# FFN gate and up products with the weight tile as the stationary operand and 256 token columns moving

## What is computed

```python
def _rmsnorm(x, g):
    y = x32 * lax.rsqrt(jnp.mean(x32 * x32, axis=-1, keepdims=True) + NORM_EPS)
    return (y * g.astype(jnp.float32)).astype(x.dtype)
def _swiglu(h, w_gate_up, w_down):
    gu = jnp.einsum('bsd,df->bsf', h, w_gate_up)
    g, u = gu[..., :FF], gu[..., FF:]
    return jnp.einsum('bsf,fd->bsd', jax.nn.silu(g) * u, w_down)
...
    for layer in range(DEPTH):
        hn = _rmsnorm(h, norm_mix[layer])
        h = h + _mixer(hn, w_in[layer], w_ret_o[layer], w_sb_o[layer], w_out[layer])
        hn = _rmsnorm(h, norm_ffn[layer])
        h = h + _swiglu(hn, w_gate_up[layer], w_down[layer])
```

## Time and profile before

| | |
|---|---|
| time before, median of 3 runs | 2092.74 us (2091.91 to 2096.03) |
| the profiled execution's own time | 2091.68 us |
| its span, first to last instruction | 2089.5 us |
| PE busy | 2070.0 us, 99% of the span |
| PE weight loads busy | 1684.9 us, 81% |
| DVE busy | 1234.4 us, 59% |
| ACT busy | 1113.5 us, 53% |
| granted TensorE clock | 1.000 of full speed |

### The profile page before, as it was taken

How to read it: one execution, slowest core, us unless ns; L and a number is a source line. 1 busy time by engine, 2 the same in 40 slices (tenths; PEclk the granted TensorE clock), 3 DMA queues, 4 the chain that set the end, 5 groups by cost and what they waited for, 6 DMA issues and landing times.

```text
span 2089.5 us, 25155 instructions
## 1 busy us (share of the span) xinstructions
PE 2070.0 (99%) x9627; PEld 1684.9 (81%) x9627; DVE 1234.4 (59%) x1721; ACT 1113.5 (53%) x1682; POOL 36.4 (2%) x60
## 2 busy tenths in 40 slices
PE   8999999999999999999999999999999999999999
PEld 7877888888778888888877888888888888788887
DVE  6576665565666655555567765655555466655553
ACT  6565444445665544644456665544444465665442
POOL 0000100000000000000000000000000000000000
PEclk9999999999999999999999999999999999999999
DMA  7545566555455665565554344565565653445553
GB/s 249 160 142 161 177 191 182 182 174 167 143 161 182 200 186 188 177 193 182 182 166 136 131 152 148 177 189 182 183 187 185 183 190 131 172 140 162 183 187 125
DMA packets 258214, 359.76 MB, mean 172 GB/s; under 512 B 16908, under 2 KB 152288, under 8 KB 258096
## 3 DMA queue, kind: packets, MB, share of 16 engines
q1 hardware_dynamic: 256016, 352.75, 53.6%
q0 software_dynamic: 2080, 5.41, 0.8%
HBM read 357.04 MB, written 1.06 MB: 171 GB/s over the span
## 4 chain that ended last, share of the span: by engine, by line
PE 96%; DVE 2%; ACT 1%; issue 1%; POOL 0%; DMA 0%; SPq 0%; DVEq 0%; ACTq 0%
PE M L780 29%; PE M L782 28%; PE M L781 28%; PE AUX L822 3%; PE AUX L836 1%; DVE WL L1270 1%; PE AUX L1022 1%; PE AUX L1000 1%; PE AUX L947 1%; ACT WH L1049 0%; PE AUX L962 0%; PE AUX L874 0%; PE AUX L953 0%; DVE RET L1453 0%; PE AUX L988 0%
## 5 line engine op out<-in xcount | busy, mean ns | idle before, releaser
L1270 DVE TENSOR_TENSOR WL<-RAW,WH 128x1024 fp32r<-128x1024 f32 x669 | 815.8, 1222 | 669.7 <-ACT WH L1049 666.9
L1049 ACT ACTIVATE WH<-RAW 128x1024 fp32r<-128x1024 f32 x669 | 706.5, 1058 | 680.7 <-PE M L782 674.8
L780 PE MATMUL M<-WH,Bh 128*128 128x512 f32 x1792 | 720.5, 402 | 2.3 <-DVE WL L1270 2.3
L782 PE MATMUL M<-WH,Bl 128*128 128x512 f32 x1792 | 700.8, 391 | 0.0
L781 PE MATMUL M<-WL,Bh 128*128 128x512 f32 x1792 | 699.1, 390 | 0.0
L782 PEld LDWEIGHTS M<-WH,Bl 128*128 128x128 f32 x1792 | 336.8, 188 | 73.2
L780 PEld LDWEIGHTS M<-WH,Bh 128*128 128x128 f32 x1792 | 337.2, 188 | 71.8 <-DVE WL L1270 3.4
L781 PEld LDWEIGHTS M<-WL,Bh 128*128 128x128 f32 x1792 | 337.8, 188 | 63.7
L1078 ACT ACTIVATE AS<-M,KEEP 128x256 f32<-128x256 f32 x132 | 55.4, 471 | 101.1 <-PE M L782 97.6
L780 PE MATMUL M<-WH,MTh 128*128 128x512 f32 x128 | 55.2, 431 | 0.0
L782 PE MATMUL M<-WH,MTl 128*128 128x512 f32 x128 | 50.6, 396 | 0.0
(11 more groups left out here) (405 smaller groups left out, 2525.1 us busy)
## 6 DMA issues: line engine op xcount, KB each, us to landing
RAW<-in_ffn_w_in SPq DMA_DIRECT2D x352, 256.0 KB, 3.2
RAW<-in_w_in SPq DMA_DIRECT2D x104, 512.0 KB, 3.5
RAW<-in_w_gate_up SPq DMA_DIRECT2D x176, 256.0 KB, 3.2
RAW<-in_ffn_w_out SPq DMA_DIRECT2D x88, 512.0 KB, 3.6
RAW<-in_w_down SPq DMA_DIRECT2D x44, 512.0 KB, 3.6
RAW<-in_x_w_kv SPq DMA_DIRECT2D x32, 512.0 KB, 3.5
RAW<-in_even_w_in SPq DMA_DIRECT2D x24, 512.0 KB, 3.8
RAW<-in_odd_w_in SPq DMA_DIRECT2D x24, 512.0 KB, 3.9
```

Of the source, the lines that this page charges most:

```text
L780: e.matmul(out, s.hi, wh, start=s.at0, stop=False)
L782: i = e.matmul(out, s.lo, wh, start=False, stop=s.final)
L1049: e.activation(p.WH[:, h, 0:s.size], p.RAW[:, i, 0:s.size], ACT.Copy).then_inc(k.w_hi, 1)
L1270: e.tensor_tensor(p.WL[:, h, 0:s.size], p.RAW[:, s.u % NRAW, 0:s.size], hi.bitcast(F32), ALU.subtract).then_inc(k.w_lo, 1)
```

## The change

The gate and up products swap their operands. For each k-tile, a 128x128 block of the weights is stationary and all 256 tokens of B move. A chunk's bank 0 gets the 256 gate features (two blocks of 128 features, 256 tokens each) and bank 1 the 256 up features, with features on the partitions. That is 8 x 4 x 3 = 96 products of 256 columns where there were 48 of 512. The result is already turned, and the four transposes of a chunk go.

Since tokens now lie along the free axis, the factor r can't be a scalar per partition any more. A new step `rb` makes one 128x256 tile RB per FFN: PE multiplies r, broadcast along the free axis, by the identity (two 128x128 products), and ACT copies the bank to RB. DVE `ff` multiplies the gate bank by RB, ACT takes its silu, DVE `fh` multiplies the up bank (without r) by it, ACT rounds to Ah, and DVE `fl` subtracts to make Al. The up half's factor r is moved behind the down products, where it is a scalar per partition again (`rs`, r times the FFN's factor of 1.0 or 0.5, in `res`). The buffers HB are changed in shape, and the memory and the final gain go into the TMP tiles, which makes room for RB.

```diff
-    "conv": (0.0, 0.9), "turn": (0.5, 1.0), "tq": (0.5, 0.0), "gains": (0.5, 1.0), "rope": (0.0, 0.6), "ff": (0.0, 0.5),
+    "conv": (0.0, 0.9), "turn": (0.5, 1.0), "tq": (0.5, 0.0), "gains": (0.5, 1.0), "rope": (0.0, 0.6), "ff": (0.7, 0.0), "fh": (0.7, 0.0), "rb": (0.4, 0.0),
...
+    def chunk_w(self, name, region, nk, lab):
...
+                for half in range(2):
+                    s = self.add("mw", self.now + 0.5 * half, 3)
+                    s.c, s.kt, s.u, s.kk, s.t, s.ncol = c, kt, u, kk, half, ncol
...
+                    s.hi, s.lo = (x[:, kt, :] for x in region)
...
-            s.c, s.half, s.scale = c, n, scale
+            s.c, s.half, s.rb = c, n, rb
...
     def ffn(self, gate, down, lab_in, lab_mid, scale, gain, lab_next, A, HB, final=False):
+        nm = self.norms[lab_in]
+        rb = self.add("rb", nm.at + 3.5)
+        rb.norm, rb.scale, rb.rs = nm, scale, self.small(T)
+        past = [None, None]
         for c_ in range(FF // 256):
-            c = self.chunk(gate, self.B, 0, KD, lab_in)
+            c = self.chunk_w(gate, self.B, KD, lab_in)
             s = self.add("ff", c.end, 0)
-            s.c, s.norm, s.i = c, self.norms[lab_in], c_
-            s.silu = [self.AS[:, (c_ % 2) * 2 + t, 0:256] for t in range(T)]
-            s.h = [HB[:, (c_ % 3) * 2 + t, :] for t in range(T)]
-            blocks = [s.h[t][:, q * P:(q + 1) * P] for q in range(2) for t in range(T)]
-            self.turn(c.end + 2.0, "bank", s, blocks, A, 2 * c_, None, lab_mid, 2 * c_)
-        self.residual(down, A, KF, lab_mid, scale, gain, lab_next, final=final)
+            f = self.add("fh", c.end + 1.2)
+            o = self.add("fl", c.end + 2.6)
+            s.c, s.rb, s.past, s.g = c, rb, past[c_ % 2], HB[:, c_ % 2, :]
+            f.c, f.s, f.past, f.h = c, s, past[c_ % 2], HB[:, 2 + c_ % 2, :]
+            o.f = f
+            f.hi, o.lo = (x[:, 2 * c_:2 * c_ + 2, :].rearrange("p k c -> p (k c)") for x in A)
+            past[c_ % 2] = o
+            for q in range(2):
+                self.made[lab_mid, 2 * c_ + q] = o
+        self.residual(down, A, KF, lab_mid, rb, gain, lab_next, final=final)
...
+        elif s.kind == "mw":
...
+            for j in range(2):
+                out = p.M[c.banks[s.t]][:, 256 * j:256 * j + 256]
+                at = s.kk * s.ncol + 256 * s.t + P * j
+                wh, wl = (x[:, h, at:at + P] for x in (p.WH, p.WL))
+                e.matmul(out, wh, s.hi, start=s.at0 and j == 0, stop=False)
+                e.matmul(out, wh, s.lo, start=False, stop=False)
+                i = e.matmul(out, wl, s.hi, start=False, stop=s.final and j == 1)
+            if s.unit_end:
+                i.then_inc(k.w_used, 1)
+        elif s.kind == "rb":
+            e.wait_ge(k.r_made, s.norm.n)
...
+            for t in range(T):
+                i = e.matmul(aux[:, t * P:(t + 1) * P], s.norm.r[:, t:t + 1].to_broadcast([P, P]), ident, start=True, stop=True)
+            i.then_inc(k.aux_full[b], 1)
...
         elif s.kind == "ff":
             table = "s"
-            for t in range(T):
-                e.activation(s.silu[t], banks[t][:, 0:256], ACT.Silu, scale=r[t]).then_inc(k.silu_made, 1)
+            e.wait_ge(k.m_out[s.c.banks[0]], s.c.use[0])
+            e.activation(s.g, s.g, ACT.Silu).then_inc(k.silu_made, 1)
+        elif s.kind == "fh":
+            e.wait_ge(k.m_out[s.c.banks[1]], s.c.use[1])
+            e.activation(s.hi, s.h, ACT.Copy).then_inc(k.ff_hi, 1)
+        elif s.kind == "rb":
+            e.wait_ge(k.aux_full[b], s.use)
+            e.activation(p.RB, aux[:, 0:T * P], ACT.Copy).then_inc(k.aux_out[b], 1)
...
         elif s.kind == "ff":
-            for t in range(T):
-                e.wait_ge(k.silu_made, 2 * (s.n - 1) + t + 1)
-                e.scalar_tensor_tensor(out=s.h[t], in0=banks[t][:, 256:512], scalar=r[t], in1=s.silu[t], op0=ALU.mult,
-                                       op1=ALU.mult).then_inc(k.m_out[c.banks[t]], 1)
...
+            e.tensor_tensor(g, m, p.RB.unsqueeze(1).to_broadcast([P, 2, T * P]), ALU.mult).then_inc(k.m_out[c.banks[0]], 1)
+        elif s.kind == "fh":
...
+            e.tensor_tensor(s.h, banks[1][:, :], s.s.g, ALU.mult).then_inc(k.m_out[c.banks[1]], 1)
+        elif s.kind == "fl":
+            e.wait_ge(k.ff_hi, s.f.n)
+            e.tensor_tensor(s.lo, s.f.h, s.f.hi.bitcast(F32), ALU.subtract).then_inc(k.ff_lo, 1)
```

More of the change, by code:

```diff
@@ L263, in chunk @@
         return c
+    def chunk_w(self, name, region, nk, lab):
+        self.bank_use[2 * self.pair] += 1
+        self.bank_use[2 * self.pair + 1] += 1
+        c = Chunk(name, self.pair, [self.bank_use[2 * self.pair], self.bank_use[2 * self.pair + 1]])
+        self.pair ^= 1
+        kt = 0
+        while kt < nk:
+            u = self.unit(name)
+            kn, ncol, _ = self.units[u]
+            for kk in range(kn):
+                for half in range(2):
+                    s = self.add("mw", self.now + 0.5 * half, 3)
+                    s.c, s.kt, s.u, s.kk, s.t, s.ncol = c, kt, u, kk, half, ncol
+                    s.at0, s.final = kt == 0, kt == nk - 1
+                    s.unit_end = half == 1 and kk == kn - 1
+                    s.src = self.made[lab, kt]
+                    s.hi, s.lo = (x[:, kt, :] for x in region)
+                    c.mms.append(s)
+                kt += 1
+                self.now += 1
+            c.done = u + 1
+        c.end = self.now
+        return c
     def unit(self, name):
@@ L643, in odd_mixer, with memory_turn @@
             self.add("cv_lo", c.end + 6.3 + 2.0 * f).y = y
-    def memory_turn(self, l, at, MX, MT):
+    def memory_turn(self, l, at, MT):
         ss = self.small(4)
         ld = self.add("memld", at)
-        ld.done, ld.MX = self.n_unit + 1, MX
+        ld.done = self.n_unit + 1
+        MX = [[self.TMP[2 * t + n] for n in range(2)] for t in range(T)]
         for n in range(2):
@@ L651, in memory_turn @@
                 k = 4 * n + 2 * j
-                blocks = [MX[:, t, (k + q) * P:(k + q + 1) * P] for q in range(2) for t in range(T)]
+                blocks = [MX[t][n][:, (2 * j + q) * P:(2 * j + q + 1) * P] for q in range(2) for t in range(T)]
                 g = [self.gain(32 + l * 40 + 24 + k + q) for q in range(2)]
                 self.turn(at + 12 + 3 * n + 1.5 * j, "mem", ld, blocks, MT, k, g, f"mt{l}_", k).kt_half = n
-            sq = self.squares(at + 13.5 + 3 * n, "mem", ld, n, [MX[:, t, n * 512:(n + 1) * 512] for t in range(T)], ss)
+            sq = self.squares(at + 13.5 + 3 * n, "mem", ld, n, [MX[t][n] for t in range(T)], ss)
         self.norm(at + 18, f"mt{l}_", sq, ss)
@@ L784, in tensor @@
                 i.then_inc(k.w_used, 1)
+        elif s.kind == "mw":
+            c = s.c
+            h = s.u % NHL
+            if s.kk == 0 and s.t == 0:
+                e.wait_ge(k.w_lo, s.u + 1)
+            if s.src not in seen:
+                seen.add(s.src)
+                e.wait_ge(k.aux_out[s.src.bank], s.src.use)
+            if s.at0 and c.use[s.t] > 1:
+                e.wait_ge(k.m_out[c.banks[s.t]], c.use[s.t] - 1)
+            for j in range(2):
[9 more added lines that the diff above has]
+            e.wait_ge(k.r_made, s.norm.n)
+            if s.use > 1:
+                e.wait_ge(k.aux_out[b], s.use - 1)
+            for t in range(T):
+                i = e.matmul(aux[:, t * P:(t + 1) * P], s.norm.r[:, t:t + 1].to_broadcast([P, P]), ident, start=True, stop=True)
+            i.then_inc(k.aux_full[b], 1)
         elif s.kind == "narrow":
@@ L1256, in vector @@
             aux = p.AUX[b]
-        if s.kind in ("ff", "ch", "res", "mer1", "mer2"):
+        if s.kind in ("ff", "fh", "ch", "res", "mer1", "mer2"):
             c = s.c
@@ L1558, in vector @@
                 x = p.X[:, t, s.half * 512:(s.half + 1) * 512]
-                q = e.scalar_tensor_tensor(out=x, in0=x, scalar=r[t], in1=p.NF[:, s.half * 512:(s.half + 1) * 512], op0=ALU.mult, op1=ALU.mult)
+                q = e.scalar_tensor_tensor(out=x, in0=x, scalar=r[t], in1=p.TMP[4 + s.half], op0=ALU.mult, op1=ALU.mult)
             q.then_inc(k.x_fin, 1)
@@ L1664, in gpsimd @@
                 for t in range(T):
-                    e.dma_start(s.MX[:, t, n * 512:(n + 1) * 512],
+                    e.dma_start(p.TMP[2 * t + n],
                                 a["mem_2"][0, t * P:(t + 1) * P, n * 512:(n + 1) * 512]).then_inc(k.d_mem[s.n - 1][n], 16)
@@ L1669, in gpsimd @@
             for n in range(2):
-                e.dma_start(p.NF[:, n * 512:(n + 1) * 512],
+                e.dma_start(p.TMP[4 + n],
                             a["norm_final"][n * 512:(n + 1) * 512].unsqueeze(0).to_broadcast([P, 512])).then_inc(k.d_nf, 16)
@@ L1788, in build_program @@
                     else:
-                        MX = sb("MXa", [P, T, D], F32, c)
-                        p.memory_turn(0, p.now, MX, MT)
-                        p.NF = MX[:, 0, :]
+                        p.memory_turn(0, p.now, MT)
```

42 lines of the change are left out of this document (30 added, 12 removed).

## The result

| | before | after |
|---|---|---|
| median of 4 runs, us | 2092.85 (2091.91 to 2096.03) | 2107.67 (2106.78 to 2109.83) |
| span of the profiled execution, us | 2089.5 | 2105.0 |

The ratio is 1.007, 95% interval 1.0052 to 1.0087. The change costs 14.8 us; the forecast was a gain of 20.5. The time is the one that the first rival, *The load takes from the stream*, gave: 2106.7 us.

The account below looks back on a forecast made before the run. PE's instruction stream was taken as the bound. Products and turns -25.2, RB +2.7, wait at `rb` +3.2 and vanished waits -1.2 gave -20.5 us: 2072.2 us from 2092.7, range 2062 to 2126, the forecast's own 2062 to 2081.

Parts of the forecast that it names:

- The load takes from the stream: Rival at every gate and up product: 120.0 ns a step, +14.0 us in all, 2106.7 us; chance 0.25.
- What bounds the kernel: PE's instruction stream: busy 2070.0 of 2089.5 us at full clock, to be read by distances from start to start.
- s: Start-to-start distance of a new 256-column gate or up product behind a full load, taken as 114.5 ns, range 111 to 126.7.
- third point: Plain float32 products on PE: nearly equal stream and full load overlap with 2 or 3 ns of loss.
- fourth: fp32r products of 384 columns behind full loads: 175 ns, 15 over the stream, which would suggest s of 120.0 ns.
- The products' and turns' term: Gate and up chunks on PE: 96 products at 114.5 ns against 11.374 us, times 66 chunks, -25.2 us.
- The argument against that rival: On gate and up products: the surcharge with hardly any load is already half of that at 512 columns.
- RB: Two plain float32 products of 128 columns per FFN on PE, 0.45 us, six times: +2.7 us.
- Wait at `rb`: PE waits once for r, in the first FFN, where POOL's DMA issues precede the norm: +3.2 us.
- Waits for HB: PE's wait in the first FFN, 0.8 us, and a smaller one in the second block go: -1.2 us.
- Turns: Four transposes per gate and up chunk on PE, with what they disturb: 0.49 us of a chunk's 11.374.
- DVE and ACT at zero: Their FFN work, at most 7.0 and 6.4 us of an 11 us chunk, was to add nothing.

Follow-up runs that it names:

- e8: Changed kernel with only 64 of 128 weight columns loaded per gate and up product in six of eight k-tiles: 2079.93 us, 113.5 ns a step.
- e7: Changed kernel with POOL's 17 DMA issues of the first FFN put behind the norm: 2102.27 us, one run.
- e4: Kernel before without the FFN's turns, ACT and DVE splitting the gated rows untransposed: 2059.76 us, ratio 0.9843.
- e5: Changed kernel with Bh and Bl moved in one 512-column product behind one load, and POOL's first-FFN DMA issues behind the norm: 2085.98 us, ratio 0.9967.
- e11: Changed kernel with only 96 of 128 weight columns loaded per gate and up product in six of eight k-tiles: 2089.93 us, 116.3 ns a step.
- e9: Kernel before with only 32 token columns loaded beside 512 moving columns in six of eight gate and up k-tiles: 2102.86 us, 231.7 ns a step.

## Why the prediction was wrong

**What bounds the kernel, and the way to read it**: right. PE sets the end in both, at full clock, and only the distance from start to start tells the time. The durations would have misled: 284 ns a product, 192 a load.

**The step that failed is the choice of s.** The prediction took 114.5 ns, "the 113.3 ns of the earlier trace rows with about half of the 2 or 3 ns that the closely matched pair in the earlier trace rows loses". It held that a full load is hidden behind a full-speed stream of 256 columns but for 1 or 2 ns. Measured are 120.0. Its third point, plain float32, was given more weight than its fourth, fp32r behind full loads. The fourth had the right number, 13.3 ns on each product; that the full load takes all of it holds for half at most (e8). The earlier trace rows is a stream at half speed; that a load hides there says nothing of a stream at full speed. The earlier trace rows is a load of 8 columns, and e8 shows that it stands for loads up to 64, not for a full one. The products' and turns' term was thus -25.2 us and came out at 66 x (11.52 - 11.374) = +9.6. The prediction gave that outcome as a rival with 0.25, though it says itself why is no test of a full load. The earlier trace rows were the rows with this type and this load, and none had less than 13 ns over the stream (13, 15 and 20).

**The argument against that rival** was that half of the surcharge is there with hardly any load. The row was right; the conclusion was not. Beside 256 columns the other half comes with the full width, and the first is paid per product too: the whole 13.3 ns doubles when a product of 512 columns becomes two.

**The other terms**: RB +2.7, measured 6 x 0.47 = 2.8. Wait at `rb`: 3.2, or 2.9 at s = 120.0; measured 2.8 on PE, and 3.1 from e7. Waits for HB, -1.2: they are gone from the list. Turns: 0.49 us a chunk with what they disturb, confirmed by e4. The sum with s = 120.0 was 2106.7, the time 2107.67. That they meet within 1 us is in part luck: in the profiled executions the six stretches and their last turns give 15.46 - 2.9 = +12.6 where the sum has +14.0, and 2.2 us of the growth of the span are the wait for the first weights, which no term had.

**DVE and ACT at zero**: right. Their new groups (xcount, busy us, mean ns, idle) on DVE:

```profile
L1410 DVE TENSOR_TENSOR HB<-M,RB 128x512 f32<-128x512 f32 x22 | 15.2, 691 | 13.1 <-PE M L839 13.1
L1415 DVE TENSOR_TENSOR HB<-M,HB 128x512 f32<-128x512 f32 x22 | 15.0, 683 | 0.5 <-ACT HB L1142 0.5
```

Bounded at 0.69 us, they took 0.691 and 0.683.

**The down products** stayed: 30 steps in 6.98 us are 232.7 ns, against 233.3.

```profile
392.53 0.40 PE L818 MATMUL M<-WH,FA0h 128*128 128x512 f32 x1
...
399.51 0.39 PE L818 MATMUL M<-WH,FA0h 128*128 128x512 f32 x1
```

**The two rules weighed.** A pair of halves costs 13.3 ns more than a whole product (240.0 against 226.7), not the 2.5 ns that follow from the table of isolated gaps in the Trainium skill, "TensorE: Matmul & The Clock Gate", section "Back-to-back issue gap"; for fp32r behind full loads these runs differ from the page, and the measurement decides. The loads' busy share is one of the two measures that the Trainium skill, "Perfetto Trace Analysis", section "Identifying the Most-Contended Engine", takes for TensorE's headroom (the other is the share of peak arithmetic). It rose from 81% to 87%. It pointed the right way, but it gives no price: if each load blocked for the 188 ns of its record, the kernel would be over 2500 us.

## What to carry to other kernels

Price a halved or doubled product by its start-to-start distance from rows of the same type and the same load; if rows of several lengths have the same surcharge over the stream, as 240 to 512 columns had here, expect it on each instruction, and halving doubles it. A row at another stream speed or with a narrow load is no substitute, however well its column count fits. To drop transposes by swapping operands, first make the moving side long enough: two moving operands with one set of weights can share its load (e5).

## What the runs showed of the hardware

The surcharge of fp32r products over their stream lay between 6.7 and 20 ns here: 6.7 to 6.8 with narrow blocks beside 256 columns, 9.6 with 96 columns (e11), 12.2 to 13.3 with full ones, and 18 to 20 in another rhythm (231.7 in e9, 233.3 in the earlier trace rows). It depends on load and stream together, and shorter loads can make it worse: e9 lost 5 ns a product against the earlier trace rows. Why a short load helps beside 256 columns and not beside 512, and why e5's rhythm changes from chunk to chunk, stays open.

A scalar read from memory was not free on DVE. The step `res` now comes in two forms, with and without one:

```profile
L1401 DVE SCALAR_TENSOR_TENSOR X<-M,SM,X 128x512 f32<-128x512 f32 x24 | 16.9, 746 | 16.1 <-PE M L820 16.1
...
L1401 DVE SCALAR_TENSOR_TENSOR X<-M,X 128x512 f32<-128x512 f32 x24 | 15.5, 686 | 6.4 <-PE M L820 6.4
```

It is 60 ns each, 24 times, hidden here behind PE; the prediction had it at nothing.
